# Token halves staggered at the layer norms of a two-layer encoder, with homes for early split weights in a shared buffer

## The chip, the cores and the metric

The kernel runs on one core of a Trainium2 chip. The metric is the device time of one execution in microseconds (us). Times of the profile are read from one profiled execution of the same kernel.

## What is computed

Two post-norm layers over 256 tokens of width 1024: layer 0 mixes tokens with a gated causal convolution, layer 1 with a latent attention of 8 heads. Each layer then runs a product-key expert mixer over all 16384 experts (selection by top 16 per head, then dense products with `u` and `v`).

```python
def layer_norm(x, g, b):
    mu = jnp.mean(xf, axis=-1, keepdims=True)
    var = jnp.mean(jnp.square(xf - mu), axis=-1, keepdims=True)
    y = (xf - mu) * lax.rsqrt(var + LN_EPS)
...
def reference(...):
    for i in range(DEPTH):
        mix = conv_module(...) if i % N_MIXERS == 0 else mla_mixer(...)
        x = layer_norm(DEEPNORM_ALPHA * x + mix, ln1_g[i], ln1_b[i])
        ff = peer(x, peer_w_q[i], peer_sub_keys[i], peer_u[i], peer_v[i])
        x = layer_norm(DEEPNORM_ALPHA * x + ff, ln2_g[i], ln2_b[i])
    return x
```

## The kernel before

**Blocks.** All large weights come as one stream of 512 KB blocks of 128x1024 (names in `STREAM`, L67): conv_in 16, conv_out 8, wq0 16, u0 128, v0 128, mla_in 6, mla_out 8, wq1 16, u1 128, v1 128. A block lands in one of three slots of `raw` (SyncE's queue, L310), ScalarE rounds it to fp32r (`high`, L694), VectorE or GpSimd takes the rest (`low` = raw - high, L336), and TensorE multiplies high by high, high by low and low by high. `high` and `low` have three slots too (`RING`), so a block can be split only when TensorE has used the block three places earlier. The next load into a slot of `raw` is issued when its low part is made.

**Two kinds of block product.** A projecting block (L405; conv_in, wq, u, mla_in) has the weights stationary and all 256 tokens moving: 24 matmuls of 256 columns into one bank of `work`. A combining block (L429; conv_out, v, mla_out) has 128 tokens stationary and the weights moving: 6 matmuls of 512 columns for each half of the tokens, 12 in all, into the four banks of `y`, half 0 in banks 0 and 1, half 1 in banks 2 and 3.

**Norms.** There are four: norm 0 after conv_out, 1 after v0, 2 after mla_out, 3 after v1. Before the first three the last three combining blocks (two before norm 2, `OUT_LAG`) run half 0 first and then half 1 (`combine_last`), and a semaphore `y_half` starts VectorE's norm of half 0 (L991/L993 to L1007, with a square root on ScalarE, L718, between). Its norm of half 1 follows once the blocks are done. Then TensorE transposes both halves (L472, 8 matmuls each, `turn_x`), ScalarE and VectorE split the transposed x into `xT_high` and `xT_low` (L725, L1017), and the next projection (wq0, mla_in, wq1) starts when half 1 is split, since its moving operand is all 256 tokens. GpSimd makes the low parts of the projection's first three blocks meanwhile.

**Convolution.** After conv_in, TensorE convolves two channel chunks with diagonal matrices (L492) that ScalarE makes (L745), VectorE five chunks (L1266), and GpSimd adds one chunk's products (L360), which ScalarE makes (L770) in one loop with the diagonals. The loop starts when the gated unit of chunk 7 (L1249, VectorE) is there.

**Attention.** Head by head, TensorE transposes probabilities (L558), makes the scores of head h+2 (L547, L549), runs the mla_out block of head h-2 (L429) and then the head's product with the values (L570). The softmax runs on VectorE and ScalarE between them.

## Time and profile before

| | |
|---|---|
| three runs | 1904.38, 1900.34, 1900.94 us (median 1900.94) |
| the profiled execution | 1901.31 us; its span, first to last instruction, 1899.1 us |
| granted TensorE clock, mean | 0.985 |
| busy | TensorE 1826.2 us (96%), VectorE 1302.4 (69%), ScalarE 925.0 (49%), GpSimd 280.1 (15%) |
| matmuls | 12338 |
| chain that ended last | TensorE 91%, VectorE 6% |

TensorE is busy nearly always, so the share by itself says little. What counts is where it is not, and how long one matmul of each kind takes from the start of one to the start of the next in a dense row: a matmul's own duration in the records (283 ns) is longer than that distance, since matmuls overlap.

### The profile page before, as it was taken

To read this page: it belongs to the slowest core of one execution; us is meant where nothing else is said; L and a number is where in the kernel's file an instruction comes from. 1 tells how busy PE (TensorE), PEld (TensorE's weight loads), DVE (VectorE), ACT (ScalarE), POOL (GpSimd) and SP (SyncE) were. 2 spreads that over 40 slices of the span, in tenths; PEclk is the share of its full clock that TensorE was granted. 3 is DMA by queue.
4 is the path that set the end of the run, shared out by engine and by line. 5 is a ranking of instruction groups with operands and counts; after the bars stand their busy time and mean duration, and the time that the engine had idled before them with its cause. 6 is when DMAs were issued, how large, how long until landed. Compare 5 with 4: busy or idle time off the path is not lost.

```text
span 1899.1 us, 31639 instructions
## 1 busy us (share of the span) xinstructions
PE 1826.2 (96%) x12338; PEld 1667.9 (88%) x12338; DVE 1302.4 (69%) x2387; ACT 925.0 (49%) x1588; POOL 280.1 (15%) x146
## 2 busy tenths in 40 slices
PE   7969999999999999999989799999999999999997
PEld 7759999999999888888877699999999988888886
DVE  6973794888965666665565539858888556666656
ACT  6654544544444555554533354445444455545453
POOL 7710657000000000000011308440000000000000
PEclk9989999999999999999989899999999999999999
DMA  7224455555556666667731355555555566666663
GB/s 247 81 89 150 151 167 173 162 156 156 157 176 204 192 196 191 196 192 256 224 103 47 98 167 168 167 166 158 157 161 160 178 203 196 193 195 192 196 192 131
DMA packets 87700, 320.05 MB, mean 169 GB/s; under 512 B 9857, under 2 KB 10369, under 8 KB 87425
## 3 DMA queue, kind: packets, MB, share of 16 engines
q1 hardware_dynamic: 84528, 307.42, 52.2%
q10 hardware_dynamic: 3024, 10.62, 1.6%
q8 instruction: 99, 1.62, 0.3%
q14 instruction: 49, 0.39, 0.1%
HBM read 316.95 MB, written 1.05 MB: 167 GB/s over the span
## 4 chain that ended last, share of the span: by engine, by line
PE 91%; DVE 6%; DMA 1%; ACT 1%; issue 1%; POOL 0%; DVEq 0%; ACTq 0%; SPq 0%
PE work L405 44%; PE y L429 38%; PE y L647 3%; PE y L492 2%; PE work L536 1%; DMA raw<-conv_in 1%; PE y L620 1%; DVE x L1000 1%; DVE x L1007 1%; DVE low L336 1%; ACT high L694 0%; DVE big L1087 0%; PE work L486 0%; POOL low L336 0%; DVE x L993 0%
## 5 line engine op out<-in xcount | busy, mean ns | idle before, releaser
L694 ACT ACTIVATE high<-raw 128x1024 fp32r<-128x1024 f32 x582 | 611.7, 1052 | 494.9 <-PE work L405 450.2
L336 DVE TENSOR_TENSOR low<-raw,high 128x1024 fp32r<-128x1024 f32 x479 | 586.4, 1225 | 320.4 <-ACT high L694 319.2
L405 PE MATMUL work<-xT_high,high 128*128 128x256 f32 x2480 | 713.2, 288 | 17.1 <-POOL low L336 10.4
L405 PE MATMUL work<-xT_low,high 128*128 128x256 f32 x2480 | 705.3, 284 | 0.0
L405 PE MATMUL work<-xT_high,low 128*128 128x256 f32 x2480 | 704.9, 284 | 0.0
L405 PEld LDWEIGHTS work<-xT_high,high 128*128 128x128 f32 x2480 | 479.5, 193 | 20.7 <-POOL low L336 10.6
L405 PEld LDWEIGHTS work<-xT_low,high 128*128 128x128 f32 x2480 | 479.7, 193 | 0.0
L405 PEld LDWEIGHTS work<-xT_high,low 128*128 128x128 f32 x2480 | 479.4, 193 | 0.0
L336 POOL TENSOR_TENSOR low<-raw,high 128x1024 fp32r<-128x1024 f32 x103 | 257.0, 2504 | 969.5 <-ACT high L694 969.3
L429 PE MATMUL y<-high,xT_high 128*128 128x512 f32 x1088 | 337.7, 392 | 6.5 <-DVE xT_low L1292 5.2
L429 PE MATMUL y<-low,xT_high 128*128 128x512 f32 x1088 | 335.9, 390 | 0.0
L429 PE MATMUL y<-high,xT_low 128*128 128x512 f32 x1088 | 335.5, 390 | 0.0
L914 ACT ACTIVATE xT_high<-big 128x256 fp32r<-128x256 f32 x256 | 106.5, 417 | 331.0 <-PE y L429 330.9
L429 PEld LDWEIGHTS y<-high,xT_high 128*128 128x128 f32 x1088 | 204.1, 188 | 49.9 <-issue 7.2
L429 PEld LDWEIGHTS y<-low,xT_high 128*128 128x128 f32 x1088 | 204.8, 188 | 42.8
L429 PEld LDWEIGHTS y<-high,xT_low 128*128 128x128 f32 x1088 | 204.6, 188 | 42.7
L1197 DVE TENSOR_TENSOR xT_low<-big,xT_high 128x256 fp32r<-128x256 f32 x256 | 108.5, 425 | 130.9 <-ACT xT_high L914 130.8
L1131 DVE TENSOR_TENSOR aux<-aux,gate 128x1024 f16<-128x1024 f16 x128 | 86.4, 716 | 0.1
L1121 DVE TENSOR_TENSOR aux<-iota,index 128x2048 f16<-128x2048 f16 x64 | 77.7, 1214 | 0.1
L647 PE MATMUL y<-aux 128*128 128x128 f16 x1024 | 68.3, 220 | 5.4 <-DVE aux L1131 5.4
L647 PEld LDWEIGHTS y<-aux 128*128 128x128 f16 x1024 | 57.3, 98 | 8.4 <-DVE aux L1131 5.8
L1266 DVE SCALAR_TENSOR_TENSOR y<-big,y 128x256 f32<-128x256 f32 x145 | 57.2, 475 | 0.0
(158 smaller groups left out, 993.3 us busy)
## 6 DMA issues: line engine op xcount, KB each, us to landing
raw<-u SPq DMA_DIRECT2D x256, 512.0 KB, 3.5
raw<-v SPq DMA_DIRECT2D x256, 512.0 KB, 4.3
raw<-wq SPq DMA_DIRECT2D x32, 512.0 KB, 3.5
raw<-conv_in SPq DMA_DIRECT2D x16, 512.0 KB, 4.6
aux<-ln_par ACTq DMA_DIRECT2D x9, 512.0 KB, 5.8
raw<-conv_out SPq DMA_DIRECT2D x8, 512.0 KB, 3.6
raw<-mla_out SPq DMA_DIRECT2D x8, 512.0 KB, 3.6
raw<-mla_in SPq DMA_DIRECT2D x6, 512.0 KB, 3.9
```

Of the source, the lines that this page charges most:

```text
L336: ops.tensor_tensor(low[:, slot, :], raw[:, slot, :], high[:, slot, :].bitcast(F32), ALU.subtract).then_inc(low_made[slot], 1)
L405: mm = nc.tensor.matmul(work[:, bank, 0:T], w[:, s, cols], m[:, k, :], start=(k == 0 and n == 0), stop=(k == KD - 1 and n == 2))
L429: mm = nc.tensor.matmul(y[:, 2 * h + m, :], a[:, a_slot, rows], v[:, s, m * 512:(m + 1) * 512], start=(start and n == 0), stop=(stop and n ...
L492: mm = nc.tensor.matmul(y[:, c, 0:T], diagonals[:, c, w, :], padded[:, k, w:w + T], start=(w == 0), stop=(w == TAPS - 1))
L536: mm = nc.tensor.matmul(work[:, j % 4, 0:T], w[:, k, :], latent_n[:, k0 + k, :], start=(k == 0), stop=(k == chunks - 1))
L647: mm = nc.tensor.matmul(y[:, 2 * q + t // 4, cols], onehots[:, q, 2, token], onehots[:, q, part, token], start=(part == 0), stop=(part == 1))
L694: A(high[:, slot, :], raw[:, slot, :], ACT.Copy).then_inc(high_made, 1)
L914: A(xT_high[:, c % RING, :], big[:, c - v0, :], ACT.Copy).then_inc(a_high, 1)
L1121: step(V.tensor_tensor(in_pairs(onehots[:, q, 1:3].rearrange("p q n -> p (q n)")), each.rearrange("p t (n d) -> p t n d", d=2), index2[:, ...
L1131: ins = V.tensor_tensor(in_pairs(onehots[:, q, part]), in_pairs(onehots[:, q, 1]), gate2[:, b, part].unsqueeze(2).to_broadcast([P, BATCH, ...
L1197: V.tensor_tensor(xT_low[:, c % RING, :], big[:, c - v0, :], xT_high[:, c % RING, :].bitcast(F32), ALU.subtract).then_inc(a_low, 1)
L1266: ins = V.scalar_tensor_tensor(conv[:, k, :] if w == TAPS - 1 else total, padded[:, k, w:w + T], tap(k, w), total, ALU.mult, ALU.add)
```

## The change

- **Tails by halves.** The last 8 combining blocks before each of norms 0, 1 and 3 run half 0 for all eight, then half 1 (`combine_tail`). Before norm 2, mla_out blocks 0 and 1 run whole within the heads, 2 to 5 only half 0 there, and the rest follows after the last head.
- **Half 0 first.** `y_half` follows half 0 of the eight. After 5 of the 8 half blocks of half 1 (after 3 of the 5 left before norm 2) TensorE transposes half 0, and ScalarE and VectorE split it.
- **Heads by halves.** The first 5 blocks of wq0, mla_in and wq1 (`HEAD_BLOCKS`) are projected for half 0 (24 matmuls of 128 columns each, `half_block`), then, after the transposes of half 1 that stand ahead of the fifth, for half 1. Results of four of them go to `y`.
- **Homes.** Blocks that must be split before they are used get homes in free rooms of `big` (`FAR`, read through `far_homes`): conv_out 3 to 7, wq 0 to 4, some of the v blocks from 104 on, mla_out 3 to 7. ScalarE and VectorE run ahead of TensorE by one block more for every four from v block 104 on (`last_high`).
- **Who splits.** Low parts of the heads' blocks: wq0 and mla_in go from GpSimd to VectorE, ahead of the norm of half 0 but for two of wq0; wq1 0 to 4 stay with GpSimd, all split during the attention. GpSimd makes the low parts of conv_out 3 to 5 too, in the convolution; ScalarE rounds those of conv_out 6 and 7 within its loop of products and diagonals.
- `w_uv` is loaded after mla_in's first block, and a's splits use 8 slots instead of 3.

```diff
+HEAD_BLOCKS = 5
+BEFORE_TURN = 4
+TAIL = 8
+TURN_AFTER = 5
+GROW_FROM, GROW_EVERY = 104, 4
...
+def last_high(c):
+
+    n = c - FIRST["v0"] if c < FIRST["mla_in"] else c - FIRST["v1"]
+    return c + RING + max(0, n - GROW_FROM + 1) // GROW_EVERY
...
-            low_stage(0, FIRST["conv_out"] + RING)
+            low_stage(0, FIRST["conv_out"] + 2 * RING)
...
+            def half_block(name, c, h, splits=None):
+
+                rows = slice(h * P, (h + 1) * P)
+                w_high, w_low = high_at(c), low_at(c)
+                if h == 0:
+                    wait_low(c)
+                for k in range(KD):
+                    if splits is not None and k % PART == 0:
+                        wait_xT(splits + k // PART)
+                    cols = slice(k * P, (k + 1) * P)
+                    for n, (w, m) in enumerate(((w_high, xT_high), (w_high, xT_low), (w_low, xT_high))):
+                        mm = nc.tensor.matmul(result(name, c)[:, rows], w[:, cols], m[:, k, rows],
+                                              start=(k == 0 and n == 0),
+                                              stop=(k == KD - 1 and n == 2))
...
+            def project_first_half(name, norm):
+
+                first, splits = FIRST[name], SPLITS_BEFORE[norm] + 1
+                for m in range(HEAD_BLOCKS):
+                    if m == BEFORE_TURN:
+                        turn_half(norm, 1)
+                    if m == 2:
+                        pe.wait_ge(var_ok, HALVES * norm + HALVES)
+                    half_block(name, first + m, 0, splits if m == 0 else None)
...
+            def combine_tail(first, norm, wait_block, whole):
+
+
+                for n in range(TAIL):
+                    wait_block(first + n)
+                    mm = combine_block(n, first + n, whole and n == 0, n == TAIL - 1, (0,))
+                mm.then_inc(y_half, 1)
+                for n in range(TAIL):
+                    if n == TURN_AFTER and norm < 2 * DEPTH - 1:
+                        turn_half(norm, 0)
+                    combine_block(n, first + n, whole and n == 0, n == TAIL - 1, (1,))
...
+                            out_half(h - OUT_LAG, (0, 1) if h - OUT_LAG < OUT_WHOLE else (0,))
                         att_mix(h)
...
+                    out_half(HEADS - 2, (0,))
+                    out_half(OUT_WHOLE, (1,))
+                    out_half(HEADS - 1, (0,)).then_inc(y_half, 1)
+                    for k in range(OUT_WHOLE + 1, HEADS):
+                        if k == OUT_TURN:
+                            turn_half(2, 0)
+                        out_half(k, (1,))
+
+                project_first_half(f"wq{layer}", 2 * layer)
+                project_second_half(f"wq{layer}", 2 * layer, range(HEAD_BLOCKS))
+                project(f"wq{layer}", HEAD_BLOCKS)
...
+            def norm_and_split(n, ready):
+
+                std(n, 0)
+                split_xT(n, 0)
+                highs_to(ready)
+                std(n, 1)
+                split_xT(n, 1)
...
+            highs_to(FIRST["conv_out"] + 2 * RING - 1)
             act.wait_ge(glu_ok, POOL_CHUNK + 1)
             for w in range(TAPS):
+                if w in (8, 16):
+                    make_high(rounded[0])
...
+                        highs_to(FIRST["mla_out"] + RING + OUT_HIGHS[h])
...
+                if layer + 1 < DEPTH:
+                    highs_to(FIRST["mla_in"] + HEAD_BLOCKS - 1)
+                    norm_and_split(2 * layer + 1, FIRST["mla_in"] + HEAD_BLOCKS)
...
+                if layer + 1 < DEPTH:
+                    low_stage(done, FIRST["mla_in"] + HEAD_BLOCKS)
```

TensorE at norm 1, from the last combining half block to the projection; `ident,x` is a transpose. Before:

```order
L429 MATMUL y<-high,xT_high 128x512 x2
L429 MATMUL y<-low,xT_high 128x512 x2
L429 MATMUL y<-high,xT_low 128x512 x2
L472 MATMUL work<-ident,x 128x128 [waits x_half_0_normalised]
L472 MATMUL work<-ident,x 128x128 x7
L472 MATMUL work<-ident,x 128x128 [waits x_half_1_normalised]
L472 MATMUL work<-ident,x 128x128 x3
L472 MATMUL work<-ident,x 128x128 [waits x_half_1_normalised]
L472 MATMUL work<-ident,x 128x128 x3
L405 MATMUL work<-xT_high,high 128x256 [waits xT_low_made,xT_high_made,low_made_2]
```

The same place of the changed kernel:

```order
L560 MATMUL work<-ident,x 128x128 [waits x_half_0_normalised]
L560 MATMUL work<-ident,x 128x128 x7
L528 MATMUL y<-far_homes,xT_high 128x512 x4
L528 MATMUL y<-far_homes,xT_low 128x512 x2
L528 MATMUL y<-far_homes,xT_high 128x512 x4
L528 MATMUL y<-far_homes,xT_low 128x512 x2
L528 MATMUL y<-high,xT_high 128x512 x2
L528 MATMUL y<-low,xT_high 128x512 x2
L528 MATMUL y<-high,xT_low 128x512 x2
L501 MATMUL y<-xT_high,high 128x128 [waits xT_low_made,xT_high_made,low_made_2]
```

The transposes of half 0 now stand ahead of three half blocks, and the projection that follows moves 128 columns, not 256.

ScalarE at the same place, from the last blocks of v0 to the root of half 0's variance (`variance_made`). Before:

```order
L914 ACTIVATE xT_high<-big 128x256 [waits block_used]
L694 ACTIVATE high<-raw 128x1024 [waits block_used,block_landed_1]
L686 ACT_TABLE_LOAD
L686 ACTIVATE warm<-ones 128x1
L718 ACTIVATE stats<-stats 128x1 [waits variance_made]
L694 ACTIVATE high<-raw 128x1024 [waits block_used,block_landed_2]
L694 ACTIVATE high<-raw 128x1024 [waits block_used,block_landed_0]
L694 ACTIVATE high<-raw 128x1024 [waits block_used,block_landed_1]
```

The changed kernel:

```order
L1018 ACTIVATE xT_high<-big 128x256 x4
L787 ACTIVATE high<-raw 128x1024 [waits block_used,block_landed_2]
L787 ACTIVATE high<-raw 128x1024 [waits block_used,block_landed_0]
L787 ACTIVATE far_homes<-raw 128x1024 [waits block_used,block_landed_1]
L787 ACTIVATE far_homes<-raw 128x1024 [waits block_used,block_landed_2]
L787 ACTIVATE far_homes<-raw 128x1024 [waits block_used,block_landed_0]
L775 ACT_TABLE_LOAD
L775 ACTIVATE warm<-ones 128x1
L813 ACTIVATE stats<-stats 128x1 [waits variance_made]
```

All five of mla_in's first blocks are now rounded ahead of that root, each after its load has landed; VectorE's low parts stand ahead of its norm of half 0 in the same way.

## Rows read from the trace of the kernel before

**Rows 1.** Waits of TensorE: engine, line, waited for, us in total, times, longest
```profile
PE work L472 <- DVE x L1007: 26.6, 6, 5.1
```
**Rows 2.** Chain that ended last, in order of time: start us, us, what
```profile
142.87 51.24 PE work L405 x408
...
194.11 7.15 PE y L620 x64
201.26 66.25 PE work L405 x552
...
346.77 0.91 PE y L647 x16
...
605.27 344.65 PE y L429 x1518
...
966.94 13.15 PE work L405 x96
...
1076.96 51.75 PE work L405 x408
```
**Rows 3.** Timeline, last combining matmuls before norm 1: start us, us, engine line op
```profile
953.39 0.61 PE L429 MATMUL y<-high,xT_low 128*128 128x512 f32 x2
```
**Rows 4.** Timeline, last combining matmuls before norms 0, 2 and 3
```profile
129.30 0.61 PE L429 MATMUL y<-high,xT_low 128*128 128x512 f32 x2
...
1062.03 0.61 PE L429 MATMUL y<-high,xT_low 128*128 128x512 f32 x2
...
1887.97 0.61 PE L429 MATMUL y<-high,xT_low 128*128 128x512 f32 x2
```
**Rows 5.** Timeline of VectorE in norm 3: first instruction of half 0 and of half 1
```profile
1884.61 1.22 DVE L993 SCALAR_TENSOR_TENSOR x<-x,y 128x1024 f32<-128x1024 f32 x1 [1.81 <-PE y L429]
...
1890.22 1.21 DVE L993 SCALAR_TENSOR_TENSOR x<-x,y 128x1024 f32<-128x1024 f32 x1
```
**Rows 6.** Instructions by line: duration ns min/median/max, first and last start us, forms
```profile
L405 PEld LDWEIGHTS work<-xT_high,high x2480: 186/192/331, 10.0 to 1538.6; 128*128 128x128 f32 x191
...
L620 PEld LDWEIGHTS y<-big x128: 190/192/193, 193.8 to 1135.5; 128*128 128x128 f32 x128
...
L558 PEld LDWEIGHTS work<-ident,big x24: 138/140/144, 1020.5 to 1053.4; 128*128 128x128 f32 x24
L558 PE MATMUL work<-ident,big x24: 272/273/333, 1020.5 to 1053.5; 128*128 128x128 f32 x24
```
**Rows 7.** Timeline, convolution; in brackets: idle before <-releaser
```profile
57.55 2.37 POOL L336 TENSOR_TENSOR low<-raw,high 128x1024 fp32r<-128x1024 f32 x1 [0.47 <-ACT high L694]
...
58.21 2.00 DVE L1249 TENSOR_TENSOR big<-big 128x256 f32<-128x256 f32 x1
...
63.66 0.41 DVE L1249 TENSOR_TENSOR big<-big 128x256 f32<-128x256 f32 x1
...
70.32 0.60 ACT L770 ACTIVATE big<-big 128x256 f32<-128x256 f32 x1 [9.39 <-DVE big L1249]
```
**Rows 8.** Waits from 45 to 106 us
```profile
PEld y L492 <- ACT big L745: 7.1, 18, 0.4
```
**Rows 9.** Instructions on raw, 900 to 950 us, columns as rows 6, and loads
```profile
L694 ACT ACTIVATE high<-raw x18: 1044/1044/1062, 900.3 to 945.9; 128x1024 fp32r<-128x1024 f32 x18
L336 DVE TENSOR_TENSOR low<-raw,high x18: 1224/1225/1226, 901.4 to 947.0; 128x1024 fp32r<-128x1024 f32 x18
...
DMA to landing us min/median/max: 3.5/4.4/7.0
```
**Rows 10.** Timeline of TensorE in the attention: transposes of heads 1, 2, 3 and 7
```profile
1024.54 0.55 PE L558 MATMUL work<-ident,big 128*128 128x128 f32 x3 [1.48 <-DVE big L1361]
...
1028.54 0.55 PE L558 MATMUL work<-ident,big 128*128 128x128 f32 x3 [1.48 <-DVE big L1361]
...
1033.64 0.49 PE L558 MATMUL work<-ident,big 128*128 128x128 f32 x3
...
1053.19 0.55 PE L558 MATMUL work<-ident,big 128*128 128x128 f32 x3 [0.47 <-DVE big L1361]
```

More of the change, by code:

```diff
@@ L410, in project_block, with project @@
                 mm.then_inc(block_used, 1)
-            def project(name, blocks=None, splits=None, skip=0):
+            def project(name, lo=0, hi=None, splits=None):
                 first = FIRST[name]
-                lo, hi = first + skip, first + (blocks or BLOCKS[name])
-                head = max(lo, min(hi, first + RING))
-                for g in range(lo, head):
-                    project_block(name, g, splits if g == first else None)
-                for g in range(head, hi):
-                    project_block(name, g)
@@ new lines, in project_first_half, with project_second_half @@
+            def project_first_half(name, norm):
[6 more added lines that the diff above has]
+                    half_block(name, first + m, 0, splits if m == 0 else None)
+            def project_second_half(name, norm, blocks):
+                first, splits = FIRST[name], SPLITS_BEFORE[norm] + PARTS + 1
+                for m in blocks:
+                    half_block(name, first + m, 1, splits if m == 0 else None)
@@ L940, in _ @@
                 act.wait_ge(emptied, PROJECTED[f"u{layer}"] + NKEYS)
-                for c in range(v0, end_of[f"v{layer}"] - RING):
+                end = end_of[f"v{layer}"]
+                for c in range(v0, end - TAIL):
                     if layer == 0 and c == v0 + TRIG_AT:
@@ new lines, in split_xT @@
+            def split_xT(n, h):
+                for part in range(PARTS):
+                    dve.wait_ge(xT_hi_ok, SPLITS_BEFORE[n] + PARTS * h + part + 1)
+                    at = (slice(None), slice(PART * part, PART * (part + 1)), slice(h * P, (h + 1) * P))
+                    V.tensor_tensor(xT_low[at],
+                                    work[:, turn_bank(n, h) + part, :].rearrange("p (k t) -> p k t", t=P),
+                                    xT_high[at].bitcast(F32), ALU.subtract).then_inc(xT_lo_ok, 1)
@@ L1277, in _ @@
             dve.wait_ge(pool_conv, 1)
+            make_low(dve, V, FIRST["conv_out"] + 2 * RING)
             dve.wait_ge(stat_mm, 1)
```

381 lines of the change are left out of this document (210 added, 171 removed).

## The prediction

> **What bounds the kernel now.** I read the page first: TensorE is busy 96% of the span and is 91% of the chain that ended last. So I looked for the time that it doesn't work, and for what one matmul costs when it does. Its waits say where: the longest in total, 26.6 us, is before the six groups of transposes, on VectorE's norm [rows 1]. But the hole at a norm is larger than that wait, since transposes and splits lie in it too. I measured it from the start of the last pair of combining matmuls plus two distances of 0.227 us: at norm 1 953.39 + 0.45 = 953.84 to the projection at 966.94, 13.1 us [rows 2, 3]; at norm 0 129.75 to 142.87, 13.1; at norm 2 1062.48 to 1076.96, 14.5 [rows 2, 4]. Together 40.7 us.
>
> After each hole the clock is low. A dense row of 256-column matmuls takes 66.25 / 552 = 0.120 us for each. The first 408 after norm 0 take 51.24 us where 408 x 0.120 = 48.96, those after norm 2 51.75, and the 96 after norm 1 13.15 where 11.52 is due [rows 2]: 2.3 + 2.8 + 1.6 = 6.7 us more.
>
> **Other distances.** A 512-column fp32r matmul takes 344.65 / 1518 = 0.227 us, so an fp32r matmul costs 0.107 us for 256 columns and 0.013 us that don't depend on them. A plain fp32 record of 128 columns takes 7.15 / 64 = 0.112, an f16 one of 128 columns 0.91 / 16 = 0.057 [rows 2].
>
> **What goes.** The tail is long enough to hide the norm. Half 1 of eight blocks is 8 x 6 x 0.227 = 10.9 us behind `y_half`; VectorE's norm of a half takes 1890.22 - 1884.61 = 5.6 us [rows 5], and the transposes stand 6.8 us after `y_half`. Their split (some 2 us) lies beside the three half blocks left, 4.1 us. The norm of half 1 (5.6 us) lies beside four half blocks of the head, 6.4 us at the cheapest price below. So the holes close but for the transposes: 48 at 0.109 us (three take 0.49 us, the last one's record 0.273 of it, so two distances are 0.217 [rows 6, 10]) are 5.2 us. At norm 3 half 1 can start when TensorE is done, 1887.97 + 0.45 + 0.2 = 1888.6, not 1890.22 behind half 0 [rows 4, 5]: 1.6 us. The gain is 40.7 + 6.7 - 5.2 + 1.6 = **43.8 us**.
>
> **What the heads cost.** Five blocks at three norms become 240 matmuls of 128 columns each time instead of 120 of 256. Half as many columns would be nearly free if only columns counted. But each matmul has its own weight load, and there are now twice as many. No fp32r matmul of under 256 columns is in the trace, so I bound it. From below: columns alone, 0.053 + 0.013 = 0.067 us, 16.0 us a head against 14.4, 4.8 us in all. From above: that a short fp32r matmul goes as slowly as a plain fp32 product, two records of 0.112, 53.6 us a head, 118 us in all. Between them stands the load. Its record lasts 192 ns for fp32r and for plain fp32, but 140 ns for a transpose of the same 128x128 [rows 6]: some 50 ns more, which is another 128 columns' time at 2.4 GHz. If the transpose's load takes 128 cycles, the fp32r load takes 256, 0.107 us, and hides under 256 moving columns but not under 128. The two nearest rows then bound the distance: 0.112 (plain fp32, 128 columns, the same load record) and 0.120 (fp32r, 256 columns). I take the middle, 0.116: 240 x 0.116 = 27.8 us a head against 14.4, 13.4 us more, **40.3 us** for three; with the two rows 37.4 to 43.2.
>
> The Trainium skill (TensorE: Matmul & The Clock Gate, LDWEIGHTS) has a load take its columns divided by 1.2, in ns, 107 ns for 128 columns, and its section on weight-path modes keeps the fast load from fp32. By that the sum would be the same as mine; what speaks against the saving in its pages is this, and the trace's record lengths agree with it, though no row shows a load that is waited for.
>
> **Convolution.** GpSimd makes three low parts more, of some 2.4 us each. Where one lay beside VectorE's gated unit, that took 2.00 us and not 0.41 [rows 7]. The one at 63.66 is now hit, and everything behind it on VectorE, the unit of chunk 7 with it, is 1.6 us late. ScalarE waits 9.39 us before its loop [rows 7], so three of the five new roundings are free. The two within the loop (1.04 us each [rows 9]) are not: TensorE waits there for diagonals 18 times [rows 8], and the stage ends with that loop. 1.6 + 2.1 = 3.7; I take 3.5 (1.5 to 5). The low parts of conv_out 6 and 7 on VectorE fall into its waits for the column sums.
>
> **Supply at norm 1.** A slot of raw turns round in a load of 4.4 us, a rounding of 1.04 and a low part of 1.22 [rows 9], with small waits 6.8 us, 2.25 us a block with three slots. Growing asks for 2.72 / 1.25 = 2.18, so it just keeps up. But when the tail begins six blocks are missing (the last of v0, five of mla_in), 13.5 us, and `y_half` comes 10.9 us later. VectorE and ScalarE have these ahead of the norm. The norm begins 2.5 to 3.5 us late, the transposes find 1.1 of it hidden (6.8 - 5.7): 2.5 us of waiting (0 to 7, by loads of 3.5 or over 5 us).
>
> **Attention.** A head with a whole mla_out block takes 1033.64 - 1028.54 = 5.1 us, one without 4.0 us, and there TensorE waits 1.48 us for the softmax; before head 7 it waits 0.47 us even with a whole block (2.7 us) as cover [rows 10]. With half a block heads 4 and 5 want 3.7 us and get 4.0, and the wait before head 7 grows by 1.4: 2 us at the least. Each head also has one or two roundings on ScalarE, 1.04 us, between the exponentials, and GpSimd's ten low parts beside the small VectorE work: up to 1 us for each head that waits, 7 in all. I take 3.5, near the lower end, since the rounding stands where ScalarE has idle time. Before norm 2 three half blocks, 4.1 us, cover a norm of 5.6 + 0.3: 1.8 us (1 to 3).
>
> **The sum.** 40.3 + 3.5 + 2.5 + 3.5 + 1.8 = 51.6 us of cost (37.4 + 4.5 to 43.2 + 22) against 43.8: 7.8 us slower, from 1.9 faster to 21.4 slower. Made against the profiled execution, 1901.3 us, which is 0.4 above the median of the runs: **1909 us**, its own range 1899 to 1923.
>
> **Rivals.**
> *Only columns count* (faster). If the load hides in another way, a half block costs 0.067 us a matmul, the heads 4.8 us, and 4.8 + 11.3 - 43.8 = -27.7: 1874 us, 1866 to 1885. For it: the additive 0.013 us is the same at 256 and 512 columns, and f16 pairs run at 0.057. Against it: those f16 loads are other loads, and 0.120 at 256 columns leaves no room to tell. The sign turns at (43.8 - 11.3 + 43.2) / 720 = 0.105 us a matmul, with the other costs as I took them. The Trainium skill (TensorE: Matmul & The Clock Gate, Back-to-back issue gap) gives 81 ns for a sustained stream of loads and 128-column matmuls; by it the heads would cost 3 x 5 = 15 us more and the time 1884. No fp32r row here has that.
> *Short fp32r is no faster than fp32.* 0.223 us a matmul: 39.2 more a head, 118 in all, 1986 us. For it: the kernel has no fp32r row of under 256 columns that would rule it out. Against: the change adds one record for each half matmul, not two.
> *The clock falls in the heads.* The array streams columns for half of the time. At 1.2 GHz the 256 cycles of a load would be 0.213 us, 240 of them 23 us a head more than mine, near 1979. Against: the distances before the change are longer only behind the holes at the norms, where TensorE had been idle [rows 2], and in the heads it is not idle.
> *The change doesn't hide the norm*, since the blocks that now stand ahead of it on VectorE are late, is the upper end of my supply term (7 us) and lies within my own range.
>
> **Chances.** Forecast 0.58, columns only 0.24, fp32 speed 0.12, low clock 0.06. The range drops the last two and holds the first two: 1868 to 1928. Faster by over 0.2% (3.8 us, about what a measurement of this kernel can tell from no change): 0.24 + 0.02 = 0.26; within it 0.13, the lower part of my own range; slower 0.61.
>
> **What would show it.** In the changed profile: the distance of the 128-column matmuls (720 of them) is the main thing; near 0.112 to 0.120 my step holds, near 0.067 the first rival, 0.22 the second. TensorE's wait for x should be near zero at norm 0, some 2 us at norms 1 and 2. The clock should stay at 1.0 through the three heads. The convolution should end some 3.5 us later, the attention heads 4 to 7 should take 4 to 5 us each with TensorE waiting ahead of the transposes of the probabilities. I am wrong if the short matmuls are fast, or if VectorE starts the norm of half 0 long after `y_half`.

## The result, and the profile after

| | us |
|---|---|
| before, median of 4 runs beside the change | 1902.4 (1900.3 to 1904.4) |
| the change, median of 4 | 1919.5 (1915.7 to 1923.4) |
| ratio, 95% interval | 1.0090 (1.0066 to 1.0114) |
| profiled execution, before and after | 1901.3 and 1923.4, spans 1899.1 and 1921.5 |

The change makes the kernel 0.9% slower. The prediction said slower, by 7.8 us, in a range up to 1928; it is slower by 17 us in the medians, twice the forecast and more, and by 22 us between the two profiled executions, of which the changed kernel's is the slowest of its four. What carried the sum holds: a matmul of 128 columns costs nearly as much as one of 256. What the forecast lacked is at the ends of v0 and v1. Intervals here and below leave out one execution, of lean_attention, that took 4648 us.

The chain that ended last in the changed kernel, start us, us, what. L528 is the combining product (L429 before), L501 a half block, L477 a whole one (L405), L716 the scores' product (L620), L628 the first product of the attention:

```profile
108.76 20.32 PE y L528 x78
...
134.08 10.67 PE y L501 x96
...
161.67 34.60 PE work L477 x288
196.27 7.15 PE y L716 x64
...
609.00 253.22 PE y L528 x1116
...
962.43 1.09 PE work L560 x8
...
969.25 10.67 PE y L501 x96
...
1001.94 22.46 PE work L628 x104
...
1145.08 7.15 PE y L716 x64
...
1557.80 302.21 PE y L528 x1332
...
1893.36 19.22 PE y L528 x72
```

Three starts of the kernel before that stand in none of its groups, from the same view of it:

```profile
105.89 19.95 PE y L429 x78
...
988.00 22.46 PE work L536 x104
...
1539.88 342.97 PE y L429 x1512
```

With [rows 2, 4] the span splits at these points. The forecast column sorts the prediction's own terms into the same stages (the 13.1 or 14.5 us hole and the cold behind it, off; 1.7 us of transposes and 13.4 of short matmuls, on):

| stage | before | after | difference | forecast |
|---|---|---|---|---|
| start to conv_out's first product | 105.9 | 108.8 | +2.9 | +3.5 |
| to the scores' product, norm 0 in it | 88.2 | 87.5 | -0.7 | -0.3 |
| to v0's first product | 411.2 | 412.7 | +1.6 | 0 |
| v0, norm 1, mla_in | 382.7 | 392.9 | +10.2 | +2.9 |
| attention, norm 2, to the scores' product | 140.7 | 143.1 | +2.4 | +3.1 |
| to v1's first product | 411.2 | 412.7 | +1.6 | 0 |
| v1 | 348.5 | 354.8 | +6.3 | 0 |
| norm 3 to the end | 10.7 | 8.9 | -1.8 | -1.6 |

Two rows differ from the forecast by more than 2 us: v0 and v1, together 13.6 of the 14.8 us that the forecast is short of the profiled span. Not every small difference is the change's. The stretches from the scores' product to v take 411.2 to 413.9 us in the profiled executions of the kernels below, so their 1.6 us are not; conv_out's first product comes at 107.9 to 109.8 us in those that have the change's convolution, so its 2.9 is good to about 1 us. The v1 stage, 354.8 here, takes 355.0 in conv_late_b and 351.8 in short_lows, which have the same code there.

What stands at the ends of v is in the waits of TensorE (engine, line, waited for: us in total, times, longest us):

```profile
PE y L528 <- DVE xT_low L1307: 7.9, 6, 2.6
PE work L650 <- DVE big L1480: 6.1, 5, 1.5
...
PE work L560 <- DVE x L1118: 5.2, 2, 3.4
```

The 26.6 us for x of [rows 1] have become 5.2 us. What has grown most is the first row, 1.3 us before: L1307 is VectorE's low part of the activations a that the combining product of v multiplies with. The same view, asked of two windows, 900 to 960 us and then 1840 to 1900 us, holds 3.5 and 3.1 us of it:

```profile
PE y L528 <- DVE xT_low L1307: 3.5, 2, 2.6
...
PE y L528 <- DVE xT_low L1307: 3.1, 2, 2.1
```

And the busy time by window says what follows each (window: us, busy us of PE, PEld, DVE, ACT and POOL, granted clock, DMA share, GB/s):

```profile
936.00:970.00 34.00, 27.14 (x113) 21.35 (x113) 20.79 (x28) 14.98 (x21) 0.69 (x2) 0.90 0.54 168
1885.00:1912.00 27.00, 23.86 (x93) 18.87 (x92) 12.40 (x18) 6.85 (x13) 0.00 (x0) 0.87 0.17 64
```

The clock is below full speed in both. Before, TensorE was busy without a break and at 1.00 up to the norm. From TensorE's timeline (start us, us, engine line op, in brackets idle before): at each end two waits lie close together, and the four 512-column matmuls behind the first take 1.17 us, those behind the second 2.04, at half the clock.

```profile
939.52 1.17 PE L528 MATMUL y<-far_homes,xT_high 128*128 128x512 f32 x4 [0.81 <-DVE xT_low L1307]
...
943.79 2.04 PE L528 MATMUL y<-far_homes,xT_high 128*128 128x512 f32 x4 [2.65 <-DVE xT_low L1307]
...
1890.68 1.17 PE L528 MATMUL y<-far_homes,xT_high 128*128 128x512 f32 x4 [2.12 <-DVE xT_low L1307]
...
1893.36 2.04 PE L528 MATMUL y<-far_homes,xT_high 128*128 128x512 f32 x4 [1.02 <-DVE xT_low L1307]
```

At v0 the second wait is the longer one, at v1 the shorter, so the length of the last wait alone doesn't tell whether the clock falls.

How the 2.65 us come about stands on the two engines ahead of TensorE. ScalarE's rounding waits for a load of v, and its a-split (941.96) stands behind that; VectorE's low part of the block waits for the rounding, and only then comes the low part of a:

```profile
941.00 1.06 ACT L787 ACTIVATE far_homes<-raw 128x1024 fp32r<-128x1024 f32 x1 [1.75 <-DMA raw<-v]
```

```profile
942.09 1.23 DVE L408 TENSOR_TENSOR far_homes<-raw,far_homes 128x1024 fp32r<-128x1024 f32 x1 [1.58 <-ACT far_homes L787]
943.23 0.42 DVE L1307 TENSOR_TENSOR xT_low<-big,xT_high 128x256 fp32r<-128x256 f32 x1
```

### The profile page after: what moved, and what is told of

It is laid out like the page before. It is cut to its first block, busy times and chain, and to the rows that moved or that the text cites. A ratio compares the mean times of both kernels' runs of the same rounds, so it can differ in the third digit from the quotient of the medians.

```text
span 1921.5 us, 32337 instructions
## 1 busy us (share of the span) xinstructions
PE 1862.9 (97%) x12698; PEld 1701.7 (89%) x12698; DVE 1288.3 (67%) x2388; ACT 926.3 (48%) x1588; POOL 274.7 (14%) x145
## 4 chain that ended last, share of the span: by engine, by line
PE 85%; DVE 7%; DMA 4%; ACT 2%; issue 1%; POOL 0%; DVEq 0%; SPq 0%; ACTq 0%
PE work L477 40%; PE y L528 33%; PE y L501 3%; PE y L743 3%; DMA raw<-v 3%; DVE y L1385 2%; PE work L628 1%; DVE low L408 1%; PE work L501 1%; PE y L716 1%; ACT high L787 1%; ACT far_homes L787 1%; PE y L580 1%; DVE far_homes L408 0%; DMA raw<-mla_in 0%
## 5 line engine op out<-in xcount | busy, mean ns | idle before, releaser
L787 ACT ACTIVATE high<-raw 128x1024 fp32r<-128x1024 f32 x518 | 545.1, 1053 | 477.4 <-PE work L477 427.9
L408 DVE TENSOR_TENSOR low<-raw,high 128x1024 fp32r<-128x1024 f32 x429 | 525.0, 1225 | 292.1 <-ACT high L787 291.1
L477 PE MATMUL work<-xT_high,high 128*128 128x256 f32 x2352 | 674.4, 287 | 16.0 <-POOL low L408 11.3
L477 PE MATMUL work<-xT_low,high 128*128 128x256 f32 x2352 | 666.8, 284 | 0.0
L477 PE MATMUL work<-xT_high,low 128*128 128x256 f32 x2352 | 666.6, 283 | 0.0
L477 PEld LDWEIGHTS work<-xT_high,high 128*128 128x128 f32 x2352 | 452.9, 193 | 18.6 <-POOL low L408 11.5
L477 PEld LDWEIGHTS work<-xT_low,high 128*128 128x128 f32 x2352 | 453.0, 193 | 0.0
L477 PEld LDWEIGHTS work<-xT_high,low 128*128 128x128 f32 x2352 | 452.6, 192 | 0.0
L528 PE MATMUL y<-high,xT_high 128*128 128x512 f32 x888 | 275.2, 391 | 6.5 <-DVE xT_low L1413 5.2
L528 PE MATMUL y<-low,xT_high 128*128 128x512 f32 x888 | 274.3, 390 | 0.0
L528 PE MATMUL y<-high,xT_low 128*128 128x512 f32 x888 | 274.3, 390 | 0.0
L528 PEld LDWEIGHTS y<-high,xT_high 128*128 128x128 f32 x888 | 167.0, 188 | 42.1 <-issue 7.2
L528 PEld LDWEIGHTS y<-high,xT_low 128*128 128x128 f32 x888 | 167.3, 188 | 35.0
L528 PEld LDWEIGHTS y<-low,xT_high 128*128 128x128 f32 x888 | 167.3, 188 | 34.8
L1307 DVE TENSOR_TENSOR xT_low<-big,xT_high 128x256 fp32r<-128x256 f32 x256 | 107.8, 424 | 112.3 <-ACT xT_high L1018 112.2
L528 PE MATMUL y<-far_homes,xT_high 128*128 128x512 f32 x400 | 112.3, 404 | 6.6 <-DVE xT_low L1307 6.6
L528 PEld LDWEIGHTS y<-far_homes,xT_high 128*128 128x128 f32 x400 | 77.0, 195 | 24.3 <-DVE far_homes L408 5.6
L787 ACT ACTIVATE far_homes<-raw 128x1024 fp32r<-128x1024 f32 x64 | 67.1, 1056 | 39.9 <-DMA raw<-v 14.9
```

The lines of the kernel that those rows point to most:

```text
L408: ops.tensor_tensor(low_at(c), raw[:, slot, :], high_at(c).bitcast(F32), ALU.subtract).then_inc(low_made[slot], 1)
L477: mm = nc.tensor.matmul(out_, w[:, cols], m[:, k, :], start=(k == 0 and n == 0), stop=(k == KD - 1 and n == 2))
L528: mm = nc.tensor.matmul(y[:, 2 * h + m, :], a[:, a_slot, rows], v[:, m * 512:(m + 1) * 512], start=(start and n == 0), stop=(stop and n == 2))
L787: A(high_at(c), raw[:, slot, :], ACT.Copy).then_inc(high_made, 1)
L1307: V.tensor_tensor(xT_low[:, (c - v0) % KD, :], big[:, c - v0, :], xT_high[:, (c - v0) % KD, :].bitcast(F32), ALU.subtract).then_inc(a_low, 1)
```

## The experiments

Each kernel is the change with the edit shown. Where an interval is given, it is for the ratio to the kernel before, run on the same chip beside it.

### The price of the short matmuls

whole_heads_b gives up the half blocks: the five blocks of each head are projected whole, behind the split of half 1. The tails and the homes stay.

```
-                for m in range(HEAD_BLOCKS):
-                    if m == BEFORE_TURN:
-                        turn_half(norm, 1)
-                    if m == 2:
-                        pe.wait_ge(var_ok, HALVES * norm + HALVES)
-                    half_block(name, first + m, 0, splits if m == 0 else None)
+                turn_half(norm, 1)
...
-                    half_block(name, first + m, 1, splits if m == 0 else None)
+                    project_block(name, first + m, splits if m == 0 else None)
```

> The change, but the first five blocks of wq0, mla_in and wq1 are projected whole (120 matmuls of 256 columns) once half 1 is split, the tails by halves and the homes kept. Theory (a half block costs almost a whole one, so the staggered heads cover the norm of half 1 with work that they add): the heads give back 3 x 12.3 = 36.9 us, three holes of half 1's norm open again, about 8 us each and 1.4 us of low clock, 28 us in all: some 9 us faster than the change, near 1911. Rival (the staggered heads pay for themselves): the holes are as long as before the change, 13 us and more, and the kernel is slower than the change, 1925.

1909.7 us (ratio 1.0042, 1.0027 to 1.0056), some 9 us faster than the change, as expected. At norm 0 the hole from the last pair (132.07 + 0.45) to the first projection at 140.55 is 8.0 us. The half of the change that overlaps the heads with the norm costs more than it hides. split_64_192_b asks what sets the price of a short matmul; it divides the 256 columns 64 to 192:

```
-                rows = slice(h * P, (h + 1) * P)
+                rows = (slice(0, 64), slice(64, T))[h]
```

> The change, with the heads' blocks cut after token 64 instead of 128: 360 matmuls of 64 columns, then 360 of 192. Theory (the weight load is the floor): both sorts stand 0.111 us apart like the 128-column ones, no shorter and no longer. Rival (a short fp32r matmul streams at half the rate, two cycles a column): 64 columns 0.058 us, 192 columns 0.165 us. The total is the same by both, within 2 us.

1960.9 us, near no theory's total, for a reason that none of them had. TensorE's timeline at the start of the first head, 64 columns each:

```profile
135.24 0.39 PE L501 MATMUL y<-xT_high,far_homes 128*128 128x64 f32 x2
135.46 0.28 PE L501 MATMUL y<-xT_low,far_homes 128*128 128x64 f32 x1
135.57 0.39 PE L501 MATMUL y<-xT_high,far_homes 128*128 128x64 f32 x2
```

Three matmuls in 0.33 us: 0.111 us, what the 128-column ones take in the change (10.67 / 96 in its chain). Half the columns and the same distance: it isn't set by the columns. But then the clock goes, though TensorE and its loads have no gap. The windows 134 to 150 and 154 to 158 us, then two rows of the timeline and one of the chain:

```profile
134.00:150.00 16.00, 16.00 (x94) 15.80 (x92) 5.65 (x10) 2.25 (x3) 0.00 (x0) 0.66 0.07 26
154.00:158.00 4.00, 4.00 (x21) 4.00 (x20) 3.84 (x5) 0.38 (x1) 0.00 (x0) 0.50 0.16 30
```

```profile
154.25 0.40 PE L501 MATMUL work<-xT_low,far_homes 128*128 128x64 f32 x1
...
154.89 0.40 PE L501 MATMUL work<-xT_low,far_homes 128*128 128x64 f32 x1
```

```profile
171.59 2.68 PE work L501 x24
```

At the lower clock three matmuls of 64 columns take 154.89 - 154.25 = 0.64 us, 0.213 each, nearly twice the 0.111; the last 24 of 192 columns, at full clock, take 2.68 us, 0.112 each. So 64, 128 and 192 columns all take 0.111 or 0.112 us, and 256 take 0.120 [rows 2]: a floor for each matmul, which nearly doubles when the clock halves. The load records grow with it, from 192 to 333 ns. It isn't a floor of every matmul, since f16 ones of 128 columns stand 0.057 us apart [rows 2]. That it is the time of the weight load is the likely reading; no run gave two matmuls one load, so other costs of an fp32r matmul are not ruled out. And the rival "the clock falls in the heads" is real at 64 columns, not at the 128 of the change, whose other two heads, 970 to 1002 and 1083 to 1145 us, also have 1.00. Its head at norm 0, same columns as the windows above:

```profile
134.00:166.00 32.00, 32.00 (x287) 32.00 (x286) 10.53 (x15) 5.56 (x11) 0.00 (x0) 1.00 0.15 50
```

### The ends of v0 and v1

short_loads_b takes the load's time away: from v block 104 on and in mla_in only a quarter of each block is fetched. It leaves out the rest of these weights, so it only measures what their transfer costs.

```
+                if (name[0] == "v" and c - FIRST[name] >= GROW_FROM) or name == "mla_in":
+                    sp.dma_start(raw[:, slot, 0:256], src[c - FIRST[name]][:, 0:256]).then_inc(landed[slot], 16)
+                    return
```

> The change, but v blocks from 104 on and mla_in are loaded only in their first 256 of 1024 columns (the rest of the slot is what stood there), so these loads are a quarter as large; no compute is left out. Theory (the turn of the three raw slots, 4 us of it the load, bounds the end of v and what stands ahead of norm 1): TensorE's waits on a's low parts at the ends of v0 and v1 (4.1 and 3.8 us) and the wait for x at norm 1 (3.4 us) go, with the low clock behind them some 15 us less than the change. Rival (ScalarE and VectorE have too much in their queues there): the waits stay within 1 us each.

1907.5 us, one run, 12 under the change where 15 were expected. v0 up to the first half block takes 960.66 - 609.56 = 351.1 us where the change takes 360.2, v1 349.0 against 354.8. Its waits, and the window in which the change stood at 0.90:

```profile
PE work L563 <- DVE x L1121: 2.6, 2, 1.8
...
PE y L531 <- DVE xT_low L1310: 1.7, 4, 0.6
```

```profile
936.00:970.00 34.00, 33.02 (x192) 28.31 (x191) 24.07 (x34) 14.04 (x21) 1.05 (x4) 1.00 0.19 58
```

So the loads are behind it: a's waits are down to short ones, and of the 2.6 us for x, 1.8 are norm 2's. a_lead asks by which path: it leaves them as they are, and lets the a-splits run six blocks ahead, not three, so that they don't stand behind roundings that wait for a load; the last of them go ahead of the tail's roundings (VectorE's a_lo in the same way).

```
+def last_a(c, end):
+
+    return min(c + RING + min(RING, max(0, c - (end - NKEYS) - 100)), end - 1)
...
-                    a_hi(c + RING)
+                    for n in range(last_a(c - 1, end) + 1, last_a(c, end) + 1):
+                        a_hi(n)
...
-                for c in range(end - TAIL + RING, end):
+                for c in range(last_a(end - TAIL - 1, end) + 1, end):
                     a_hi(c)
+                for c in range(end - TAIL + RING, end):
                     highs_to(min(last_high(end - TAIL - 1) + c - (end - TAIL + RING) + 1, end - 1))
```

> The change, with one thing altered: near the end of v0 and v1 ScalarE and VectorE split the activations a of up to six blocks ahead instead of three (from block 101 on), and the last of them before the tail's roundings instead of between them. In the changed kernel TensorE waits 7.9 us for a's low parts, 4.1 at the end of v0 and 3.8 at the end of v1, and the clock is low behind both. Theory (the a-splits stand behind roundings that wait for loads, while the v blocks themselves are there): the wait disappears at both ends; at v1 that gives 3.8 us and 1 to 2 of clock, at v0 nearly nothing, since VectorE still has the five mla_in blocks ahead of the norm, so that TensorE waits for x longer instead: 1913 to 1915 us against 1919.5 for the change. Rival (the loads alone bound the end of v0 and v1): the wait only moves from a's low parts to the low parts of v, 1917 to 1920.

1917.5 us (1.0078, 1.0061 to 1.0095): 2 us under the change, a time that the rival had and not the theory. The trace shows the theory's mechanism all the same: no wait for the low parts of v has come in its place. v1 is one dense row again, first row below, 1536 matmuls at 0.227 us: 6.3 us of the stage have gone. At norm 1 nothing came of it: from v0's first product to the attention's first it takes 1003.04 - 609.53 = 393.5 us, and 392.9 in the change. The wait moved to x, second row, and the norm starts where it did, since two loads of mla_in stand ahead of it in the chain, with their roundings and low parts. The rows are of three views: the chain, the waits, and the chain again.

```profile
1558.84 348.46 PE y L533 x1536
```

```profile
PE work L565 <- DVE x L1125: 10.7, 2, 8.9
```

```profile
943.68 4.15 DMA raw<-mla_in
...
950.24 4.58 DMA raw<-mla_in
...
957.07 1.23 DVE x L1111
```

Of the 6.3 us at v1 the medians show only 2; the profiled executions differ by 1923.4 - 1918.1 = 5.3. Part of the reason is that the stage without the edit takes 351.8 to 355.0 us (above) and the change's profiled execution stands near the upper end; with the edit it is 348.5 in each of the four kernels that have it and the growing lead. The four runs of each spread over 4.4 and 7.6 us, so how much the medians should show stays open. Two limits lay on one another at norm 1: the a-parts held TensorE, the loads of five mla_in blocks held the norm.

whole_lead takes both away. It is whole_heads_b with a_lead's edit, and without any mla_in block ahead of the norm, which whole heads don't need so early:

```
-                    highs_to(FIRST["mla_in"] + HEAD_BLOCKS - 1)
-                    norm_and_split(2 * layer + 1, FIRST["mla_in"] + HEAD_BLOCKS)
+                    highs_to(end - 1)
+                    norm_and_split(2 * layer + 1, end + RING - 1)
...
-                if layer + 1 < DEPTH:
-                    low_stage(done, FIRST["mla_in"] + HEAD_BLOCKS)
+                low_stage(done, end)
...
                     split_xT(n, 0)
+                    low_stage(end, end + RING)
```

> The kernel whole_heads_b (tails and homes of the change, but the five head blocks projected whole behind half 1's split) with two things altered: the a-splits lead by six near the end of v as in a_lead, and ahead of norm 1 ScalarE and VectorE have no mla_in block to make (three between the halves' norms, the rest behind). whole_heads_b takes 1909.7, waits 9.6 us for a's low parts, and has the clock low behind. Theory (all of this is queueing, not loads): 9.6 + 1 to 2 of clock go, and the norm at norm 1 starts right behind y_half: 1896 to 1900 us, at or under the kernel before (1901 to 1902). Rival (the loads bound v's ends, also without the staggered heads): 1905 to 1909.

1897.8 us (0.9973, 0.9962 to 0.9984): 12 us under whole_heads_b and 0.3% faster than the kernel before. The 9.6 us for a's low parts have become 1.3, v1 is dense (1536 matmuls in 348.4 us), and what is left is the norms' second half:

```profile
PE work L559 <- DVE x L1119: 18.5, 4, 6.2
...
PE y L527 <- DVE xT_low L1308: 1.3, 2, 0.6
```

Of the profiled difference 3.5 us are at v1, where only the order of the a-splits can have done it, and 8.7 from v0's first product to the first projection behind norm 1; how these divide between the order and the mla_in blocks no run tells.

Its timeline at norm 0 prices the other side of the staggered heads:

```profile
133.87 0.61 PE L527 MATMUL y<-far_homes,xT_low 128*128 128x512 f32 x2
139.73 1.97 PE L559 MATMUL work<-ident,x 128*128 128x128 f32 x8 [5.24 <-DVE x L1119]
142.35 0.55 PE L482 MATMUL y<-xT_high,far_homes 128*128 128x256 f32 x1 [0.65 <-ACT xT_high L818]
```

The hole from the last pair's start plus two distances to the first projection is 142.35 - 134.32 = 8.0 us; the low clock behind it costs 1.5 more (its 408 matmuls take 50.5 us where 408 x 0.120 = 49.0). That is what half blocks of the head could hide, 9.5 us, for which the change pays 161.67 - 134.08 = 27.6 us for five blocks in place of 14.4: 13.2. The staggered heads with both limits taken away were not run; by this price, 3.7 us a norm, they would stand some 11 us above whole_lead, an estimate.

whole_no_growth is whole_lead with `GROW_FROM, GROW_EVERY = 104, 1000`, so that the roundings keep three blocks ahead at all times.

> whole_lead without the growing lead of the roundings (three blocks ahead at all times, not one more every four blocks from v block 104). It tells what the thirteen homes' lead is worth once the heads are whole. Theory: the tail takes a v block every 1.36 us in its first half, the supply gives one every 2.25; with three ahead the eighth comes 5 x 2.25 = 11.3 us after the tail's start where it is wanted at 9.5, so TensorE waits 1.7 us at each end, for low parts of v: 3 to 4 us slower than whole_lead. Rival (the growth itself costs, since it makes the engines wait for loads): 2 us or more faster than whole_lead.

1906.6 us (1.0017, 1.0008 to 1.0027), 9 us slower than whole_lead. The mechanism is there, TensorE waits for low parts of v at both ends, but it costs more than twice what I worked out. The waits of 930 to 960 us, then those of 1860 to 1895 us, where 0.5 more is for a low part in `low`:

```profile
PE y L527 <- DVE far_homes L413: 2.2, 2, 1.3
```

```profile
PE y L527 <- DVE far_homes L413: 2.0, 3, 1.2
```

I had 1.7 at each end; 2.2 and 2.5 are there. The stages tell more than the waits. From v0's first product to the transposes of half 1 it takes 962.76 - 603.31 = 359.5 us against 962.02 - 605.50 = 356.5 in whole_lead, and v1 takes 352.9 against 348.5: 7.4 us together, with the clock at 1.00 at both ends. The waits' rows hold 4.7 of them; at v1 the timeline has further gaps of 0.2 to 0.3 us, too short for these rows. The profiled executions are only 5.2 us apart because the stretches ahead of v0 were 2.2 us shorter in this one. So the growing lead, which I had taken as what starves the end of v, is worth its place: what starved TensorE was the order of the a-parts behind it and the five early mla_in blocks.

### Convolution

conv_late_b takes out the two roundings within ScalarE's diagonal loop and makes the low parts of conv_out 6 and 7 behind the chunk splits:

```
-                if w in (8, 16):
-                    make_high(rounded[0])
...
-            make_low(dve, V, FIRST["conv_out"] + 2 * RING)
             dve.wait_ge(stat_mm, 1)
...
-            make_low(dve, V, FIRST["conv_out"] + 2 * RING + 1)
             dve.wait_ge(stat_mm, 2)
...
+            make_low(dve, V, FIRST["conv_out"] + 2 * RING)
+            make_low(dve, V, FIRST["conv_out"] + 2 * RING + 1)
             dve.wait_ge(x_in, 16 * HALVES)
```

> The change, but the roundings and low parts of conv_out 6 and 7 come after the convolution's chunks are split, as late as conv_out needs them. Theory: conv_out starts 2.0 us earlier than in the change (106.8 and not 108.8 us), since ScalarE's loop is 2.1 us shorter; the other 0.8 us over before stays. Rival (GpSimd's low parts hold up VectorE's gated units, and that is the whole delay): it still starts at 108.8.

1925.2 us, one run, so in time nothing. conv_out starts at 106.23 in place of 108.76, 2.5 us earlier, 0.3 behind the kernel before. Of these, 0.7 are there before the edit can act, since ScalarE's loop starts at 70.65 and not at 71.39; 1.8 are the two roundings'. But the scores' product comes at 195.54, only 0.7 ahead: the two blocks' late lows hold wq's loads, which now stand in the chain (113.42, 3.73 us, and 119.56, 4.24). So the two roundings do delay the stage, and taking them away gives the gain back at the norm.

### Attention

whole_out4 is whole_lead with `OUT_WHOLE` 4 in place of 2, so that heads 4 and 5 have a whole block as cover again.

> whole_lead with four mla_out blocks whole instead of two. Heads 4 and 5 get back 1.36 us of cover each, the norm behind the attention loses two half blocks of cover, 2.7 us. My term for the attention (the heads are slower because the cover is gone, 2 of 3.5 us): the attention heads 4 to 7 become 2 to 3 us shorter, the wait for x at norm 2 grows from 1.8 to about 4.5: within 1.5 us of whole_lead. Rival (the heads are slower because of the roundings and GpSimd's low parts): the heads stay as they are, 2.5 to 3 us slower than whole_lead.

1903.9 us (1.0009, 0.9998 to 1.0020), 6 us slower than whole_lead: worse than either. VectorE's timeline before the last head shows why, and GpSimd's beside it:

```profile
1050.18 1.41 DVE L1480 TENSOR_SCALAR big<-big 128x128 f32<-128x128 f32 x1
1051.51 2.51 DVE L1482 TENSOR_SCALAR big<-big 128x256 f32<-128x256 f32 x1
```

```profile
1049.15 7.11 POOL L413 TENSOR_TENSOR far_homes<-raw,far_homes 128x1024 fp32r<-128x1024 f32 x3 [2.66 <-ACT far_homes L786]
```

The two scalings of the probabilities take 0.28 and 0.35 us elsewhere. Here they end at 1051.6 and 1054.0, which is when GpSimd's first and second low part of 2.37 us end (1051.5 and 1053.9), to 0.1 us. TensorE waits 4.0 us in front of the transposes, and the granted clock is 0.50 from 1054 to 1058 us. In the change itself the same stands before head 4 (VectorE, then GpSimd):

```profile
1051.75 2.28 DVE L1478 TENSOR_SCALAR big<-big 128x128 f32<-128x128 f32 x1
```

```profile
1049.21 4.73 POOL L408 TENSOR_TENSOR far_homes<-raw,far_homes 128x1024 fp32r<-128x1024 f32 x2 [4.41 <-ACT far_homes L787]
```

The Trainium skill (SBUF — State Buffer, SBUF: two separate sides) says that GpSimd and some operations of VectorE (those in a mode that uses two ports, or, against a GpSimd operation that reads SBUF, those with two inputs from SBUF) take a shared pair of ports for a whole instruction, and whoever comes second is blocked meanwhile. These ends agree with it; that the scalings, which have one input, run in such a mode, the trace doesn't show.

short_lows measures it in the change: GpSimd's ten low parts of the attention are cut to 128 columns, and TensorE multiplies with the high part in their place.

```
+                        nc.gpsimd.tensor_tensor(low_at(c)[:, 0:128], raw[:, slot, 0:128],
+                                                high_at(c)[:, 0:128].bitcast(F32),
+                                                ALU.subtract).then_inc(low_made[slot], 1)
```

> The change, with the ten low parts that GpSimd makes beside the attention cut from 1024 columns to 128 (and TensorE multiplying with the high part in their place, so that the output is not the reference's: this only measures what the ten cost). The attention, from the first product behind the mla_in head to the end of the combine, takes 80.9 us in the change and 74.5 before. Theory (VectorE waits for GpSimd): the stage falls by 2 to 4 us, and the waits in front of the transposes of the probabilities, 6.1 us in five, fall to 3 or less. Rival (the missing cover of half blocks): they stay at 5 to 6 us and the stage within 1 us of 80.9.

The stage takes 1081.58 - 1003.46 = 78.1 us against 80.9 (one run), and the waits are those of the kernel before, 3.4 us in three:

```profile
PE work L659 <- DVE big L1489: 3.4, 3, 1.5
```

So GpSimd's low parts cost 2.8 us, as the theory has it. The kernel before had 74.5; 1.1 us of transposes of half 0 and the 1.78 us of waiting for x at norm 2 (the chain has the transposes at 1079.04) are new in the change, and 80.9 - 2.8 - 1.1 - 1.8 - 74.5 = 0.7 us are left for the missing cover. That is a remainder and not a measurement.

lean_attention builds on that: whole_lead with five of GpSimd's low parts moved to VectorE, two between the splits of norm 2 and three behind them; ScalarE rounds at most one block behind each head (not shown).

```
-                    low_stage(FIRST["mla_out"] + RING, FIRST["wq1"] + HEAD_BLOCKS)
+                    low_stage(FIRST["mla_out"] + RING, end_of["mla_out"])
...
+                if layer == 1:
+                    low_stage(FIRST["wq1"], FIRST["wq1"] + 2)
                 layer_norm(n, 1, end, bias_in=(layer == 0))
                 split_xT(n, 1)
+                if layer == 1:
+                    low_stage(FIRST["wq1"] + 2, FIRST["wq1"] + HEAD_BLOCKS)
```

> whole_lead with GpSimd's five low parts of wq1 taken away from the attention's last heads: two are made by VectorE between the splits of the two halves at norm 2, three behind it, and ScalarE rounds at most one block behind each head. In the traces a VectorE operation that lies beside one of GpSimd's low parts ends when that low part ends (1.41, 2.28 and 2.51 us where it takes 0.28 to 0.35 alone, each in front of transposes that TensorE waits for). whole_lead takes 1897.8 us. Theory (that is what the heads 4 to 7 pay, not the missing cover): two such waits, 1.3 to 2 us each, go, and nothing takes their place at norm 2, where VectorE has 4 us free between the halves: 1893 to 1896 us. Rival (cover): the wait in front of the transposes stays, since the exponentials are what it waits for, and the lows behind norm 2 cost 1 to 2 us in the projection of wq1: 1898 to 1900.

1896.8 us (0.9965, 0.9953 to 0.9976), not to be told from whole_lead's 0.9973. The waits before the transposes fall from 6.1 to 4.9 us, less than the two whole waits that the theory had going, and the norm of half 1 now has two low parts ahead of it and starts late: from the attention's first product to wq1's first it takes 1076.22 - 987.66 = 88.6 us, whole_lead 1074.59 - 985.75 = 88.8. The time is just above the 1893 to 1896 of the theory, and the run decides nothing: no gain worth its lines.

## Why the prediction was right and where it was short

The sign and the main term were right. The size was short: 17 us in the medians where 7.8 were forecast. The median, 1919.5, lies near the upper end of the forecast's own range (1899 to 1923). That 1868 to 1928 holds the result says little, since it also holds the rival at 1874.

**The heads: right.** 0.116 us a matmul between bounds of 0.112 and 0.120; it is 0.111, just under the lower row, and 240 of them take 26.7 us where I had 27.8, 36.9 us more for three heads where I had 40.3. The stage with norm 0 changed by -0.7 us against -0.3. 64, 128 and 192 columns all stand at one price, as a floor by the load would have it. The step from the record lengths in [rows 6] to that floor is only argued: transposes, whose load records are shorter (140 ns), stand 0.109 us apart too, so the record length alone doesn't set the distance. The Trainium skill (TensorE: Matmul & The Clock Gate, Back-to-back issue gap) has 81 ns for a stream of short matmuls, which would have given 1884; the trace has 111 for these, and the measurement decides.

**The holes: right.** Wait for x 26.6 to 5.2 us, none at norm 0, 1.78 at norm 2 (1.8 said), 3.4 at norm 1 (2.5 said, but see the supply below). Norm 3 gave 1.8 (1.6 said).

**Convolution: right** in size, 2.9 against 3.5, and in place: 1.1 us because ScalarE's loop starts late, where I had 1.6, and 1.8 for the two roundings, where I had 2.1. VectorE's gated units, 0.41 us in [rows 7], took 2.26 and 1.35 us beside GpSimd's low parts. The loop waits for the second, chunk 7's, which starts at 70.01 where it started at 69.87: the 1.85 us that the first lost don't show there, since in this execution it began 1.7 us earlier than before. The same rows of the change:

```profile
61.95 2.26 DVE L1368 TENSOR_TENSOR big<-big 128x256 f32<-128x256 f32 x1
...
70.01 1.35 DVE L1368 TENSOR_TENSOR big<-big 128x256 f32<-128x256 f32 x1
```

**Attention: right in the sum, by luck.** 3.5 us said and 3.5 taken. But I had put 2 at the least on the missing cover and the rest on small delays near the low end; short_lows gives 2.8 to GpSimd's low parts, and 0.7 are left for the cover.

**Supply: the step that failed.** I gave it 2.5 us (0 to 7), all at norm 1, all as a late norm. Two things were wrong in it.

The late norm is a larger term than that. In the change TensorE waits only 3.4 us for it, but there TensorE is late itself. a_lead, where TensorE is dense to the end of the tail, shows the term alone: half 0 of the eight is done at 946.96, the norm begins at 957.07, 10.1 us behind and not 2.5 to 3.5, and TensorE waits 8.9 us for x, above my 7. (In the change's v0 stage the term comes to 2.5 + 7.3 = 9.8 us, waits and low clock together.) The price of a block was right, the count of the blocks was not. The tail begins at 609.53 + 1440 x 0.227 = 936.4; between there and 957.07 nine blocks are still rounded and split, four of v0 and five of mla_in, at 2.3 us each (2.25 said), where I had counted six. So "it just keeps up" is what failed: from 901.0 to 936.7 us the roundings of the change come every 2.38 us (15 in 35.7), and growing asks for one in 2.18.

And I followed the v blocks only, and not what is queued behind a rounding that waits for its load: the a-split of the same iteration, on ScalarE and then on VectorE. That holds TensorE for 3.5 us at the end of v0 and for 3.1 at the end of v1, with the low clock behind both. At v0 it costs nothing in the end, since the norm is later still: a_lead takes it away and the stage stays as long. At v1 no block stands ahead of the norm, and it is the whole 6.3 us, where I had no term at all, since I had tied supply to mla_in. Short loads and a_lead show it from two sides: without the load's time neither end waits long, and with the a-parts ahead of the roundings v1 is dense with all loads as they were.

With 6.3 us at v1 and 7.3 more in the v0 stage than its term, 1909 becomes 1923, the profiled execution. The median lies 4 us under that.

## What to carry to other kernels

Splitting a stationary-heavy product into halves of its moving columns can cost nearly the full price for each half; work out first at how many columns the matmul stops getting cheaper, here between 192 and 256 for fp32r. Before letting one stream run further ahead, list what each engine does behind the instruction that will now wait: a cheap step for another operand (here the a-splits) belongs ahead of it. Where supply and demand are within some per cent of one another (2.25 us a block against 2.18), count the blocks that will be missing from the slower rate, and not from the plan. And use an overlap only where its cover is free: the tails and homes without the staggered heads, with this order mended, were 0.3% faster than the kernel before, and the whole change 0.9% slower.

## What the runs showed of the hardware

- An fp32r matmul with its own 128x128 weight load takes 0.111 to 0.112 us at 64, 128 and 192 columns, 0.120 at 256, 0.227 at 512. At the lower of the two clocks the 64-column ones take 0.213 us and their load records 333 ns, not 192: the floor goes by TensorE's clock.
- Dense rows of 64-column fp32r matmuls lost the clock (0.66 granted over the first 16 us, 0.50 behind them) although neither TensorE nor its weight loads had a gap; rows of 128 columns at the same distance kept 1.00. To shorten the moving side can cost the clock as well. That surprised me most.
- A VectorE operation of 0.28 to 0.41 us beside a GpSimd low part took up to 2.51 us, and ended 0.1 to 0.3 us behind the end of that low part.
- Two waits close together in a dense row, 0.81 and 2.65 us at v0, 2.12 and 1.02 at v1, were followed by matmuls at half speed, behind the second wait and not behind the first (four 512-column matmuls in 2.04 us, not 1.17). The longer of the two was the second at v0 and the first at v1.
